# An encoder layer with 32 experts on one core: dynamic passes from pass 29, the last norm's rows broadcast by GpSimd, last passes and last transfer rearranged

## What is computed

```python
logits = (x @ w_router + b_router).astype(jnp.float32)
top_v, top_i = lax.top_k(logits, TOP_K)          # 4 of 32
gates = jax.nn.softmax(top_v, axis=-1)
...
for e in range(N_EXPERTS):
    hid = x @ w_up[e] + b_up[e]                  # 1024 -> 2048
    x_glu = jnp.minimum(hid[..., ::2], SWIGLU_LIMIT)
    x_lin = jnp.clip(hid[..., 1::2], -SWIGLU_LIMIT, SWIGLU_LIMIT)
    act = x_glu * jax.nn.sigmoid(SWIGLU_ALPHA * x_glu) * (x_lin + 1.0)
    out = out + gate_full[:, e:e + 1] * (act @ w_down[e] + b_down[e])
...
h = layer_norm(DEEPNORM_ALPHA * h + ffn, ln2_g[l], ln2_b[l])
```

## Time and profile before

| what | value |
|---|---|
| median of three runs | 1073.86 us (1073.74 to 1074.52) |
| the profiled execution: its time, its span | 1072.99 us, 1071.2 us |
| TensorE busy, share of the span | 1034.8 us, 97% |
| VectorE, ScalarE, GpSimd busy | 276.0, 207.1, 10.1 us |
| read from HBM, over the span | 426.03 MB, 399 GB/s with the writes |
| mean granted TensorE clock | 0.987 of full speed |

### The profile page before, as it was taken

How to read it: one execution, slowest core, us unless ns; L and a number is a source line. 1 busy time by engine, 2 the same in 40 slices (tenths; PEclk the granted TensorE clock), 3 DMA queues, 4 the chain that set the end, 5 groups by cost and what they waited for, 6 DMA issues and landing times.

```text
span 1071.2 us, 13106 instructions
## 1 busy us (share of the span) xinstructions
PE 1034.8 (97%) x5236; PEld 457.7 (43%) x5236; DVE 276.0 (26%) x717; ACT 207.1 (19%) x385; POOL 10.1 (1%) x27
## 2 busy tenths in 40 slices
PE   8999999999999999999999999999999999999997
PEld 8988784333333333333333333333333333334332
DVE  6888673111111111111111111011111111211043
ACT  5665421111111111111110111111111111011141
POOL 2000000000000000000000000000000000000000
PEclk9999999999999999999999999999999999999999
DMA  9583799999999999999999999999999999999996
GB/s 327 154 220 128 299 410 415 424 428 426 434 429 431 426 428 430 429 431 432 432 431 434 432 426 435 433 429 433 433 432 431 432 433 431 431 431 424 425 425 263
DMA packets 38624, 427.87 MB, mean 399 GB/s; under 512 B 4256, under 2 KB 17616, under 8 KB 20576
## 3 DMA queue, kind: packets, MB, share of 16 engines
q1 hardware_dynamic: 36864, 426.65, 95.2%
q10 hardware_dynamic: 1568, 0.44, 0.2%
q0 software_dynamic: 160, 0.32, 0.1%
HBM read 426.03 MB, written 1.57 MB: 399 GB/s over the span
## 4 chain that ended last, share of the span: by engine, by line
PE 73%; DMA 26%; DVE 1%; ACT 0%; issue 0%; POOLq 0%; ACTq 0%; DVEq 0%
PE bank L1866 29%; DMA pool_f<-in_w_down_dram 25%; PE bank L1932 16%; PE bank L1770 4%; PE bank L1489 4%; PE bank L1755 4%; PE bank L1506 3%; PE bank L1564 2%; PE bank L1763 2%; PE bank L1916 2%; PE bank L1880 1%; PE bank L1902 1%; PE bank L1534 1%; PE bank L1951 1%; PE bank L1470 0%; PE bank L1464 0%
## 5 line engine op out<-in xcount | busy, mean ns | idle before, releaser
L1866 PE MATMUL bank<-pool_f,bench 128*64 128x512 f32 x2048 | 453.6, 594 | 0.0
L1866 PEld LDWEIGHTS bank<-pool_f,bench 128*64 128x64 f32 x2048 | 144.1, 137 | 264.6 <-issue 255.7
L1932 PE MATMUL bank<-pool_f,bench 128*64 128x512 f32 x992 | 230.6, 619 | 23.3 <-DMA pool_f<-in_w_down_dram 23.3
L1932 PEld LDWEIGHTS bank<-pool_f,bench 128*64 128x64 f32 x992 | 75.6, 142 | 174.1 <-issue 152.5
L797 ACT ACTIVATE bench<-bench 128x256 f32<-128x256 f32 x64 | 26.6, 418 | 429.9 <-DVE bench L1342 429.9
L1342 DVE TENSOR_SCALAR bench<-bank 128x256 f32<-128x256 f32 x64 | 26.9, 420 | 296.5 <-PE bank L1866 296.5
L1324 DVE TENSOR_SCALAR bench<-iota_s,keyp,bench 128x128 f32<-128x128 f32 x62 | 18.6, 343 | 319.2 <-PE bank L1902 319.0
L1770 PE MATMUL bank<-bench,putT 64*128 64x512 f32 x248 | 61.6, 615 | 0.0
L1755 PE MATMUL bank<-X,bench 128*64 128x512 f32 x248 | 58.7, 592 | 0.0
L802 ACT COPY bench<-bank 128x512 f32<-128x512 f32 x31 | 18.2, 587 | 201.6 <-PE bank L1932 201.6
L1333 DVE TENSOR_SCALAR bench<-iota_s,keyp 128x64 f32<-128x64 f32 x60 | 12.5, 251 | 97.9 <-PE bank L1866 97.9
(11 more groups left out here) (323 smaller groups left out, 697.5 us busy)
## 6 DMA issues: line engine op xcount, KB each, us to landing
pool_f<-in_w_up_dram SPq DMA_DIRECT2D x41, 4096.0 KB, 30.3
pool_f<-in_w_down_dram SPq DMA_DIRECT2D x23, 4096.0 KB, 33.2
pool_f<-in_w_up_dram SPq DMA_DIRECT2D x40, 2048.0 KB, 19.8
pool_f<-in_w_down_dram SPq DMA_DIRECT2D x12, 2048.0 KB, 17.0
pool_f<-in_w_up_dram SPq DMA_DIRECT2D x12, 1024.0 KB, 9.9
pool_f<-in_w_down_dram SPq DMA_DIRECT2D x12, 1024.0 KB, 23.8
wbuf<-in_w_in_dram SPq DMA_DIRECT2D x9, 1024.0 KB, 8.5
bench<-in_w_in_dram SPq DMA_DIRECT2D x2, 1024.0 KB, 8.4
```

The source lines that it names most:

```text
L1866: ins = mm(bank[n][c * SLOTS:(c + 1) * SLOTS, :], xT[:, k, :], units(row, n, c), start=(k == 0), stop=(k == KT - 1))
L1932: ins = mm(bank[2][c * SLOTS:(c + 1) * SLOTS, :], actT[:, at:at + SLOTS], wk[:, a * D + c * 512:a * D + (c + 1) * 512], start=(i == 0 and ...
```

## The change

- FIXED becomes 29: pass 29 is dynamic too, its w_up and w_down come as single chunks and halves, and the fixed homes are those of passes 29 and 28. PLANNED stays 28, so no static pass is left between the long loop and the last static piece.
- ends_met is called behind pass 28's first product, ahead of pass 28's turn_over. Its results are waited for in act_turned(28). ScalarE's three copies go ahead of its pass 28.
- put_back and gates_turned leave turn_over and form back(p), which stands at the head of the dynamic loop for the pass before. The sequencer's increments, the load of last_pass and the loop's set-up come ahead of it. Behind the loop, back runs once more without gates_turned.
- ln2_g and ln2_b come as two rows of 4 KB into one partition, right behind the static chunks, and GpSimd broadcasts them to all partitions. ScalarE's copies of the state wait for it, as the rows lie in their place.
- The last chunk comes in three pieces (1/2, 1/4, 1/4), the last of which only the last two matmuls wait for. moments_paired(0) moves into the last chunk's product, behind its first half.
- In the output projection, tile 0 with the attention half and tile 1 with the recurrent half run both column halves in one step: high and low input with the high weights for both, then the low weights for both. VectorE norms tile 0 ahead of tile 1's first sum.

```diff
-        FIXED = NE - 2
+        FIXED = NE - 3
...
-            sp.wait_ge(s["chunk_used"], used(down_at(FIXED - 2, DNC - 1)))
+            sp.wait_ge(s["chunk_used"], used(SMALLER - 1))
             for i, v in enumerate((ln2_g, ln2_b)):
-                sp.dma_start(ln2p[:, i, :], v[0].partition_broadcast(P)).then_inc(s["ln2_in"], 16)
+                sp.dma_start(ln2row[:, i * D:(i + 1) * D], v[0:1, :]).then_inc(s["ln2row_in"], 16)
...
-            for c in range(DNC):
-                load_down(sp, LAST_HOME[c], e, c, s[f"last_in{c}"])
+            load_down(sp, LAST_HOME[0], e, 0, s["last_in0"])
+            for i, there in enumerate((chunk_in[LAST_HOME[1]], s["last_in1"], s["last_in2"])):
+                w = slice((0, 2, 3)[i] * D, (2, 3, 4)[i] * D)
+                sp.dma_start(buffer(LAST_HOME[1])[:, w], source(e, UPC + 1)[:, w]).then_inc(there, 16)
...
+            pool.wait_ge(s["ln2row_in"], 32)
+            g.partition_broadcast(lncat[:, 0:2 * D], ln2row).then_inc(s["ln2_in"], 1)
...
-            expert_pass(PLANNED)
             act.wait_ge(s["ends_ps"], 1)
...
-            with act.Fori(PLANNED + 1, last_pass) as p:
+            with act.Fori(PLANNED, last_pass) as p:
                 expert_pass(p)
+            act.wait_ge(s["ln2_in"], 1)
...
-            summed(1, 0)
             normed(0, 0)
             normed(0, 1)
+            summed(1, 0)
...
-                first, middle, final = (0, 2, 1) if t == part_ else (0, 1, 2)
-                for i in (first, middle, final):
+                if n == BOTH:
+                    order = ((0, 0), (2, 0), (0, 1), (2, 1), (1, 0), (1, 1))
+                else:
+                    order = ((0, n), (1, n), (2, n))
+                for i, m in order:
...
-                    if i == 2 and t == part_ and n == 1:
+                if n == BOTH and (i, m) == (2, 1):
                         ins.then_inc(s["high_used"], 1)
...
+            def back(p, final=False):
+
+                put_back(p, final)
+                if not final:
+                    gates_turned(p)
...
-            pe.wait_ge(s["ends_in"], 3)
+            ends_met()
             turn_over(FIXED - 1)
...
             with pe.Fori(FIXED, last_pass) as p:
+                back(p - 1)
                 hidden(p)
                 turn_over(p)
+            back(last_pass - 1, final=True)
             hidden(last_pass, {3: lambda: state_gathered(0), 5: lambda: state_gathered(1)})
```

More of the change, by code:

```diff
@@ L174, in encoder_layer @@
         ln2p = lncat[:, 0:2 * D].rearrange("p (i n) -> p i n", i=2)
+        ln2row = late[0:1, 0:2 * D]
         kpad = lnp[:, 0, :].rearrange("p (g o n) -> p g o n", g=NG, o=2)
@@ L299, in encoder_layer @@
         BATCH = [(t, g) for t in range(TT) for g in range(NG)]
+        BOTH = 2
         def two(kind, b):
@@ L849, in _ @@
             preload(ACT.Sqrt)
-            act.wait_ge(s["ln2_in"], 32)
+            act.wait_ge(s["ln2_in"], 1)
             for c in range(2):
@@ L1392, in state_normed @@
             def state_normed():
-                dve.wait_ge(s["ln2_in"], 32)
+                dve.wait_ge(s["ln2_in"], 1)
                 for t in range(TT):
@@ L1539, in mix_out @@
             def mix_out(t, part_, n):
-                if part_ == 0 and n == 0:
+                if part_ == 0 and n in (0, BOTH):
                     pe.wait_ge(proj_read[GI["zg" if t == 0 else "ih"]], 1)
@@ L1562, in mix_out @@
                         pe.wait_ge(s["att_low_ready"], 2 - t)
+                    final = order[-2 + m][0] if n == BOTH else 2
                     for k in range(4):
-                        ins = mm(bank[4 + 2 * t + n][:, :], cp[:, k, :], wp[:, k * D + n * 512:k * D + (n + 1) * 512],
-                                 start=(part_ == 0 and i == first and k == 0), stop=(part_ == 1 and i == final and k == 3))
-                    if i == 2 and t == part_ and n == 1:
+                        ins = mm(bank[4 + 2 * t + m][:, :], cp[:, k, :], wp[:, k * D + m * 512:k * D + (m + 1) * 512],
+                                 start=(part_ == 0 and i == 0 and k == 0), stop=(part_ == 1 and i == final and k == 3))
+                    if n == BOTH and (i, m) == (2, 1):
                         ins.then_inc(s["high_used"], 1)
-                if part_ == 1:
-                    ins.then_inc(s["mix_done"], 1)
-                elif n == 1:
+                    if part_ == 1 and i == final:
+                        ins.then_inc(s["mix_done"], 1)
+                if part_ == 0 and n in (1, BOTH):
                     ins.then_inc(s["mix_half"], 1)
@@ L1764, in gather_turned, with scatter @@
                 ins.then_inc(s["xT_ps"], 1)
-            def scatter(start=False, stop=False, rows_of=ysb):
+            def scatter(start=False, final=False, rows_of=ysb):
                 for q in range(4):
                     r = slice((q % 2) * SLOTS, (q % 2 + 1) * SLOTS)
-                    mm(bank[4 + q][:, :], putT[r, (q // 2) * P:(q // 2 + 1) * P], rows_of[r, :], start=start, stop=stop)
+                    ins = mm(bank[4 + q][:, :], putT[r, (q // 2) * P:(q // 2 + 1) * P], rows_of[r, :], start=start, stop=final)
+                if final:
+                    ins.then_inc(s["put_ps"], 1)
             def ends_met():
-                pe.wait_ge(s["actT_ready"], PLANNED + 1)
+                pe.wait_ge(s["actT_ready"], PLANNED)
                 pe.wait_ge(s["ends_ready"], 1)
@@ L1893, in put_back @@
                 else:
-                    scatter(stop=not isinstance(p, int) and turn is None)
+                    scatter(final=final)
                 if isinstance(p, int) and p == RESIDUAL:
@@ L1912, in act_turned @@
             def act_turned(p):
+                if isinstance(p, int) and p == PLANNED:
+                    pe.wait_ge(s["ends_in"], 3)
                 pe.wait_ge(s["act_ready"], 2 * p + 2)
@@ L1948, in last_down @@
                             pe.wait_ge(s[f"last_in{i}"], 16)
+                        if i == 1 and a == 3:
+                            pe.wait_ge(s["last_in2"], 16)
                         at = a * P + i * SLOTS
@@ L1955, in last_down @@
                             first_on_second()
+                        if i == 1 and a == 1:
+                            moments_paired(0)
                     ins.then_inc(s["chunk_used"], 1)
-                    if i == 0:
-                        moments_paired(0)
-            MET_AT = KT - 1
             def turn_over(p, turn=None, nth=0):
@@ L1967, in turn_over @@
                 gather_turned(p + 1)
-                put_back(p, turn)
-                gates_turned(p)
+            def back(p, final=False):
+                put_back(p, final)
+                if not final:
+                    gates_turned(p)
             def expert_pass(p, turn=None, nth=0):
                 turn_over(p, turn, nth)
-                ends = {MET_AT: ends_met} if isinstance(p, int) and p == PLANNED else {}
-                hidden(p + 1, ends, turn=turn, nth=nth + 1)
+                back(p)
+                hidden(p + 1, turn=turn, nth=nth + 1)
             keep_warm(bank[0], 2)
```

10 lines of the change are left out of this document (5 added, 5 removed).

## The result

| | before | changed |
|---|---|---|
| median of the timed executions | 1074.24 us (6: 1073.74 to 1075.32) | 1082.45 us (6: 1080.07 to 1085.43) |
| ratio to before | | 1.0081, interval 1.0068 to 1.0093 |
| profiled execution, its span | 1072.99, 1071.2 us | 1085.43, 1083.7 us |
| TensorE idle ahead of its first matmul | 1.88 us | 13.90 us |
| idle before the put-back L1781 (L1770 before) | none | 1.66 us |

The change makes the kernel slower by 0.81%, four times what this measurement can tell from no change. The forecast was 1071.9 us with a range up to 1074.8: wrong in size and in sign. The cause stands neither in the forecast nor among the rivals.

The account below looks back on a forecast made before the run. DMA bounds the kernel up to the last wait for weights at 989.23 us, TensorE behind it. Terms -0.9 - 0.95 + 0.1 - 0.4 + 0.2 = -1.95 us take 1073.86 to 1071.9 us; range 1069.5 to 1074.8.

Parts of the forecast that it names:

- The last norm's rows: GpSimd's broadcast replaces two 512 KB transfers: at least 2.1 us, up to 40 us covered, so 0 effect.
- Rival (3): GpSimd's broadcast takes over 40 us and delays ScalarE's state copies; at 55 us the kernel takes some 1082; 4%.
- The sequencer's gap: Pass 28, before the put-back: TensorE's increments, load and loop set-up no longer hidden, +1.9 us, bounds 0 and 2.4.
- Rival (2): The sequencer's work before pass 28's put-back stays hidden, so the 1.9 us don't arise: 1070.0 us, 14%.
- Rival (1): TensorE's clock falls once more, in a full product behind ends_met: 1073.6 us, 32%; a second fall: 1075.3 us, 6%.
- The 0.60 from 988 to 991 us: Mean granted TensorE clock around the second product at 989.23, read as half the stretch at 1.2 GHz.
- the 0.8 us before 989.23: TensorE's wait ahead of that second product, taken as for ScalarE's three copies; moves behind the product and costs nothing.
- Pass 28 to 29: Second product starts at 989.7 instead of 989.23, clock kept; the next at 1016.3 instead of 1017.25: -0.95 us.
- Last passes: Pass 30's gate transposes go, -0.4 us; moments_paired(0) moved into the last weights' middle delays VectorE, +0.2 us.
- Prologue: Output projection's new order frees high weights earlier, two transfers issue 0.9 us earlier: -0.9 us, bounds 0 and -1.1.
- Rival (4): The output projection's new order gives nothing, as a later TensorE wait sets the stream's start again: 1072.8 us, 4%.
- The sum: All terms over the whole kernel: -1.95 us, taking the median from 1073.86 to 1071.9 us.

Follow-up runs that it names:

- the broadcast alone: Kernel before, and of the change only the last norm's two rows brought by GpSimd's broadcast: 1085.19 us, ratio 1.0105.
- the changed kernel with the iota alone: Changed kernel plus one iota of 128x2 on an unread tile, issued on GpSimd behind the broadcast: 1073.97 us, ratio 0.9994.
- the one with the old order: Changed kernel with the last norm's rows by two broadcasting transfers and the output projection's products in the order of before: 1072.59 us, ratio 0.9988.
- the one with the affine_select: Changed kernel plus a memset and an affine_select of 128x2 on an unread tile, on GpSimd behind the broadcast: 1086.19 us, ratio 1.0095.
- the rows by transfers: Changed kernel, but the last norm's two rows come by two broadcasting transfers and GpSimd broadcasts nothing: 1073.54 us, ratio 0.9997.
- both repairs: Changed kernel with an iota behind GpSimd's broadcast and TensorE's increments and last_pass load moved ahead of ends_met: 1070.49 us, ratio 0.9965.

## Why the prediction was wrong, and where it was right

**The last norm's rows: wrong, and enough for the whole miss.** The step was "up to 40 us are covered, so 0". It priced the broadcast's own duration (2.1 us at least; it took 2.30) and its lateness (near 990; 998 less the 12 us of the start is 986), and both held. What failed is the premise that an instruction costs where it stands. The price fell due at 1.5 us of the next execution: 11.4 us with the broadcast alone. The forecast took its price from a memset, ahead of which no configuration step stands, and so from the duration alone. The Trainium skill's rule told above (GPSIMD Engine Reference, 2.1: a first call to freshly loaded code pays a load) would have raised the question, and two rows of the kernel before bore on it: the configuration step ahead of its first affine_select and the 0.24 us behind it, which say that this program asks for its code at the start and finds it there. Neither was read.

**Rival (3), slower by a late broadcast,** ended on the right side by the wrong mechanism. It needed a broadcast of over 47 us.

**The sequencer's gap: right.** 1.9 us were forecast before the put-back of pass 28, with bounds 0 and 2.4; it is a little less, 1.64 to 1.66 us in each of the five profiles that have this order of code, and gone when the work is moved ahead. Rival (2), hidden work, falls.

**Rival (1), the clock: it came true more often than not, and should have been the forecast.** Behind ends_met the product took 8.7 us or more in six of the eight profiles with ends_met in pass 28, and 7.09 in the other two (the changed kernel with the iota alone, and the one with the old order). The forecast gave a fall 38%, although six of the eight long waits that it counted had ended in one. In the changed kernel's profile the clock fell a second time, at the gap (0.55 from 985 to 988 us), and likewise in the one with the affine_select; in the other three with the gap it did not. What decides between the cases was not found: a wait for weights of 0.75 to 0.80 us ahead of pass 27's product stands in cases of either kind.

**Two readings of the rows.** The 0.60 from 988 to 991 us was read as "half of it ran at 1.2 GHz". A mean of 0.60 between 1.0 and 0.5 is four fifths of the stretch, 2.4 of 3 us; the sum doesn't use it. And the 0.8 us before 989.23 was called ScalarE's, where the row names DMA: in the kernel with the new order of the output projection alone, where the weights are in by then, this product starts 0.56 us earlier and waits 0.43 us for ScalarE's copies:

```profile
988.67 8.66 PE L1938 MATMUL bank<-pool_f,bench 128*64 128x512 f32 x32 [0.43 <-ACT late L845]
```

**Pass 28 to 29.** The forecast put the second products at 961.0, 989.7 and 1016.3. With the rows by transfers, where the start is undisturbed, they are at:

```profile
959.06 8.78 PE L1945 MATMUL bank<-pool_f,bench 128*64 128x512 f32 x32
...
972.64 1.99 PE L1779 MATMUL bank<-bench,putT 64*128 64x512 f32 x8 [1.66 <-issue]
...
989.14 7.04 PE L1945 MATMUL bank<-pool_f,bench 128*64 128x512 f32 x32
...
1015.76 7.04 PE L1945 MATMUL bank<-pool_f,bench 128*64 128x512 f32 x32
...
1062.17 0.70 DVE L1432 BATCH_NORM_STATS2 late<-bank 128x6 f32<-128x512 f32 x1
```

The first is 1.9 us earlier than forecast, 1.7 us of it because the clock had not fallen in pass 27 (7.09 us for the product where before it was 8.78), the third 0.5 us earlier. The two errors nearly cancel: the clock took 1.7 us in pass 28 instead of in pass 27.

**Last passes: right in sum, one term misplaced.** From the second product of pass 30 to the end of the last product it is 46.36 us (1015.76 to 1062.12) where it was 46.48 (1017.25 to 1063.73): -0.12 against the -0.4 + 0.2 of the sum. The gates' transposes give -0.37. The +0.2 is +0.25 on TensorE, in the products that moments_paired now divides; VectorE is not late: its last norm starts 0.05 us behind the last product in both kernels.

**Prologue.** Forecast -0.9. The earlier issue holds, and in part the fuller gaps of DMA (some 0.6 us by 200 us); "the 0.9 us arrives at the end" does not show: landings 0.15 to 0.66 us earlier, where profiles of one kernel differ by 1.27, and no measured gain. Rival (4) with its 4% was too cheap.

**The sum** without the rows was -1.95 us, or -0.25 with one fall of the clock. Measured without the broadcast: -0.3 us by the medians (interval -1.3 to +0.75). So the forecast with rival (1) comes near for everything but the one edit that it set at zero, and that one cost 11.4 us by itself. The parts don't add up exactly: 1073.86 - 0.3 + 11.4 is 1085.0, and the changed kernel's median is 1082.45. The chance of 0.35 for "faster" doesn't follow from its terms either; two fifths of 40% and the 14% give 0.30. The remark that the two transfers less "would pay if TensorE got ahead of DMA in the last 70 us" came true, for about half of the 2.4 us, in the kernel with both repairs. A wait for weights behind 989 us, which the prediction had named as a sign of being wrong, showed in three runs with the rows by transfers.

## What to carry to other kernels

Price an engine instruction of a kind that the kernel has not used yet by its duration, by what must be set up ahead of it, and by the state that it leaves: an execution in a series begins with what the last one left. In the profile, look for configuration steps ahead of it and ahead of the engine's first instruction, and after the change read the first 15 us as carefully as the place of the edit. An experiment that is to put a state back must show in its own trace that it did.

## What the hardware showed that was not expected

- GpSimd's change of code takes 7.4 to 7.6 us in mid-kernel (DMA at 428 GB/s from 988 to 996 us) and 11.4 to 12.3 us at the start of an execution (343 GB/s from 1.6 to 13.5 us). The configuration steps themselves show as 10 to 130 ns each; the rest is "issue".
- Affine_select ran under the code that the broadcast had brought, 0.07 us behind the instruction before it; ahead of the iota stood a configuration step and 7.4 to 7.6 us of idle time.
- The forward change, from the set-up's code to the broadcast's (at 173.7 us), shows no cost: GpSimd waited there for 825 us anyway.
- A broadcast of one row of 2048 elements to 128 partitions takes 2.30 us on GpSimd.
